# Fourth layer's attention with values standing and turned weights moving, two heads beside each other

## The reference

```python
def odd_mixer(h, w_qkv, q_norm, k_norm, rel_table, w_out):
    q, k, v = jnp.split(h @ w_qkv, 3, axis=-1)
    q = rms_norm_2(split_heads(q, N_HEADS_CHUNK), q_norm)
    k = rms_norm_2(split_heads(k, N_HEADS_CHUNK), k_norm)
    o = chunk_band_attention(q, k, split_heads(v, N_HEADS_CHUNK), rel_table)
    return merge_heads(o) @ w_out

# in chunk_band_attention, for every chunk:
        sc = jnp.einsum('bhqd,bhkd->bhqk', q_c, k_band, preferred_element_type=F32) * scale + bias
        ...
        p = jax.nn.softmax(jnp.where(valid[None, None, None, :], sc, -jnp.inf), axis=-1)
        return jnp.einsum('bhqk,bhkd->bhqd', p.astype(v.dtype), v_band)
```

## Time and profile before

| | us |
|---|---|
| median of 3 runs | 2021.64 |
| lowest, highest | 2015.75, 2021.70 |
| the profiled execution | 2018.59 |
| its span | 2016.8 |
| fourth layer's attention, first scores to the first matmul of the output projection | 620.14 to 646.84 of the span |

### The profile page before, as it was taken

The page is one execution under the profiler, slowest core; times in us unless marked ns, Lnnn a source line. Parts: engine busy times, 40 slices in busy tenths (PEclk is TensorE's granted clock), DMA queues, the critical chain, the costliest instruction groups (busy, mean ns, idle before and its releaser), DMA issues.

```text
span 2016.8 us, 25907 instructions
## 1 busy us (share of the span) xinstructions
PE 1937.1 (96%) x9513; PEld 1597.2 (79%) x9513; DVE 1523.1 (76%) x1723; ACT 1267.1 (63%) x1393; POOL 90.6 (4%) x99
## 2 busy tenths in 40 slices
PE   4999998999999899999999999999999999999997
PEld 3887887888887688888888888888888877778876
DVE  6657765544577789889898888989889884467775
ACT  2544675534455577878777787877778765445553
POOL 0000210000000320000000000000000000100001
PEclk8999998999999999999999999999999999999999
DMA  9774645555552399999999999999999995624400
GB/s 356 238 248 136 211 150 186 178 197 179 170 193 86 130 412 372 379 385 365 386 363 381 374 379 379 362 392 363 381 385 368 379 357 167 209 64 151 169 1 32
DMA packets 186268, 535.12 MB, mean 265 GB/s; under 512 B 12609, under 2 KB 23893, under 8 KB 186198
## 3 DMA queue, kind: packets, MB, share of 16 engines
q1 hardware_dynamic: 179952, 518.95, 70.2%
q10 hardware_dynamic: 4422, 8.92, 1.2%
q0 software_dynamic: 1824, 6.31, 1.2%
HBM read 521.02 MB, written 13.12 MB: 265 GB/s over the span
## 4 chain that ended last, share of the span: by engine, by line
PE 85%; DVE 7%; ACT 4%; DMA 2%; issue 1%; ACTq 0%; DVEq 0%; POOL 0%; SPq 0%
PE bank L456 25%; PE bank L458 24%; PE bank L457 24%; DVE WL L1164 3%; ACT WH L1160 2%; PE bank L654 2%; PE bank L643 1%; DMA ring<-in_od_we_down 1%; PE bank L2706 1%; PE bank L364 1%; DVE P L1148 1%; PE bank L428 1%; PE bank L669 1%; PE bank L667 1%; PE bank L665 1%
## 5 line engine op out<-in xcount | busy, mean ns | idle before, releaser
L1164 DVE TENSOR_TENSOR WL<-ring,WH 128x2048 fp32r<-128x2048 f32 x475 | 1072.0, 2277 | 261.9 <-ACT WH L1160 258.2
L1160 ACT ACTIVATE WH<-ring 128x2048 fp32r<-128x2048 f32 x475 | 901.9, 1912 | 363.8 <-PE bank L458 336.4
L456 PE MATMUL bank<-WH,XTH 128*128 128x512 f32 (+1 forms) x1872 | 740.4, 396 | 16.1 <-DVE XTL L1941 6.5
L458 PE MATMUL bank<-WH,XTL 128*128 128x512 f32 (+1 forms) x1872 | 729.4, 390 | 0.0
L457 PE MATMUL bank<-WL,XTH 128*128 128x512 f32 (+1 forms) x1872 | 729.1, 389 | 0.0
L456 PEld LDWEIGHTS bank<-WH,XTH 128*128 128x128 f32 x1872 | 353.9, 189 | 102.1 <-DVE WL L1164 21.6
L458 PEld LDWEIGHTS bank<-WH,XTL 128*128 128x128 f32 x1872 | 353.7, 189 | 73.9
L457 PEld LDWEIGHTS bank<-WL,XTH 128*128 128x128 f32 x1872 | 354.1, 189 | 68.9 <-issue 0.2
L456 PE MATMUL bank<-WH,HTH 128*128 128x512 f32 (+1 forms) x568 | 219.9, 387 | 1.0 <-DVE WL L1164 0.8
L458 PE MATMUL bank<-WH,HTL 128*128 128x512 f32 (+1 forms) x568 | 217.9, 384 | 0.0
L457 PE MATMUL bank<-WL,HTH 128*128 128x512 f32 (+1 forms) x568 | 217.7, 383 | 0.0
(11 more groups left out here) (442 smaller groups left out, 1371.1 us busy)
## 6 DMA issues: line engine op xcount, KB each, us to landing
ring<-in_od_we_gate SPq DMA_DIRECT2D x112, 1024.0 KB, 7.3
ring<-in_od_we_up SPq DMA_DIRECT2D x112, 1024.0 KB, 8.2
ring<-in_od_we_down SPq DMA_DIRECT2D x112, 1024.0 KB, 8.0
ring<-in_w_in SPq DMA_DIRECT2D x20, 1024.0 KB, 5.7
ring<-in_fox_w_in SPq DMA_DIRECT2D x16, 1024.0 KB, 6.9
ring<-in_nsa_w_in SPq DMA_DIRECT2D x14, 1024.0 KB, 5.1
ring<-in_w_ada SPq DMA_DIRECT2D x12, 1024.0 KB, 10.1
ring<-in_ev_w_in SPq DMA_DIRECT2D x12, 1024.0 KB, 5.2
```

The costliest lines, as they stand in the source:

```text
L456: nc.tensor.matmul(out, x[0], wt[0][:, k, :], start=start, stop=False, skip_group_check=check)
L458: return nc.tensor.matmul(out, x[1], wt[0][:, k, :], start=False, stop=stop, skip_group_check=check)
L1160: nc.scalar.activation(wh, slot_ap(n, nk, width), ACT.Copy).then_inc(hi_made, 1)
L1164: nc.vector.tensor_tensor(wl, slot_ap(n, nk, width), wh.bitcast(F32), ALU.subtract).then_inc(lo_made, 1)
```

## The change

Three things change, all in the fourth layer's attention.

First, the operands of the weighing change places. The values of a head, 128x64, stand as the loaded operand, and its turned weights move: 256 columns for the first 128 keys, 128 for the second. The output is then already turned, with the head's 64 columns on the partitions. The first head of a pair writes partitions 0 to 63 of a bank, the second 64 to 127, so a pair gives one finished slice of 128 rows and 256 tokens of the projection's input. `TO4` goes away: ScalarE copies the slice to XTH (line 817) and VectorE makes XTL (line 841), pair by pair.

Second, the tokens are now on the free axis of the output, so the division can't come after it as one factor per partition. The exponentials are divided before they are turned: VectorE takes the reciprocals of a pair (line 832, signal `inverted`), and GpSimd multiplies the three blocks of each head in place in E (line 824, signal `evened`), two instructions a head. The transposes (line 775) wait for `evened` in place of `exped`.

Third, the lists change. TensorE issues for each p the scores, the transposes of both heads of pair p-1, and then the weighing of pair p-2 (lines 788 and 792). VectorE issues the reciprocals of pair p-1, the maxima of pair p, the copies of pair p-1, and XTL of pair p-3. The output projection is one product over four chunks that waits for the slices.

```diff
+        class TurnedAttention(Attention):
...
+            def turn(self, pe, j):
+
+                pe.wait_ge(evened, j + 1)
+                if j >= 2:
+                    pe.wait_ge(copied, self.u + j - 1)
+                for c in range(3):
+                    last = nc.tensor.transpose(bank[6 + j % 2][:, c * 128:c * 128 + 128],
+                                               self.E[j % 4][:, c * 128:c * 128 + 128], ident[:, :])
+                last.then_inc(turned, 1)
+
+            def weigh_pair(self, pe, p):
+
+                pe.wait_ge(copied, self.u + 2 * p + 2)
+                if p >= 4:
+                    pe.wait_ge(turn_dve, self.bd + p - 3)
+                for kt in range(TT):
+                    for a in range(2):
+                        w_, out = PT[a], bank[p % 4][64 * a:64 * a + 64, :]
+                        if kt == 0:
+                            nc.tensor.matmul(out[:, 0:S], self.units[2 * p + a][2](0),
+                                             w_.rearrange("p (b s) -> p b s", b=3)[:, 0::2, :], start=True, stop=False,
+                                             skip_group_check=True)
+                        else:
+                            nc.tensor.matmul(out[:, 128:S], self.units[2 * p + a][2](1), w_[:, 128:256], start=False,
+                                             stop=True, skip_group_check=True).then_inc(valued, 1)
+
+            def pe(self, pe):
+                N = self.n
+                for p in range(N + 2):
+                    if p < N:
+                        self.scores(pe, p)
+                    if 1 <= p <= N:
+                        for a in range(2):
+                            self.turn(pe, 2 * (p - 1) + a)
+                    if p >= 2:
+                        self.weigh_pair(pe, p - 2)
+
+            def act(self, act):
...
+                    if p >= 3:
+                        act.wait_ge(valued, self.u + 2 * (p - 3) + 2)
+                        nc.scalar.activation(XTH[:, p - 3, :], bank[(p - 3) % 4][:, 0:S], ACT.Copy).then_inc(turn_act, 1)
+
+            def pool(self, pool):
+                for i in range(len(self.units)):
+                    pool.wait_ge(inverted, i // 2 + 1)
+                    for t0, (a, n) in enumerate(((0, 128), (128, 256))):
+                        e = self.E[i % 4][:, a:a + n]
+                        last = nc.gpsimd.tensor_scalar(e, e, rr[:, t0, i % 8:i % 8 + 1], None, ALU.mult)
+                    last.then_inc(evened, 1)
+
+            def dve(self, dve):
+                for p in range(self.n + 3):
+                    if 1 <= p <= self.n:
+                        uu = (2 * p - 2) % 8
+                        dve.wait_ge(exped, self.u + 2 * p)
+                        nc.vector.reciprocal(rr[:, :, uu:uu + 2], rs[:, (p - 1) // 4, :, uu:uu + 2]).then_inc(inverted, 1)
+                    for a in range(2):
+                        if p < self.n:
+                            self.highest(dve, 2 * p + a)
+                    for a in range(2):
+                        if 1 <= p <= self.n:
+                            self.copy(dve, 2 * (p - 1) + a)
+                    if p >= 3:
+                        dve.wait_ge(turn_act, self.ba + p - 2)
+                        nc.vector.scalar_tensor_tensor(out=XTL[:, p - 3, :], in0=bank[(p - 3) % 4][:, 0:S], scalar=1.0,
+                                                       in1=XTH[:, p - 3, :].bitcast(F32), op0=ALU.mult,
+                                                       op1=ALU.subtract).then_inc(turn_dve, 1)
...
-            A4.pe(pe, lambda a: (pe.wait_ge(grouped, A4.g + 1), TO4[0].pe(pe, first=a, end=a + 1)))
-            TO4[0].wait(pe)
-            OUT4[0].pe(pe, last_=False, late=lambda: (A4.wait(pe), TO4[1].pe(pe)))
-            OUT4[1].pe(pe, first=False, operand=TO4[1], closes=True, between=early_tiles(pe, 3, T5))
+            A4.pe(pe)
+            OUT4.pe(pe, operand=A4, closes=True, between=early_tiles(pe, 3, T5))
```

More of the change, by code:

```diff
@@ L750, in bank_of, with __init__, sums, wait_tiles @@
                 return bank[g % 2 * 2 + tt][:, :].rearrange("p (u d) -> p u d", d=self.dv)
+        class TurnedAttention(Attention):
+            def __init__(self, units, bias, bias_ready):
+                self.spare_ready, self.pe_mask = None, None
+                self.units, self.bias, self.bias_ready = units, bias, bias_ready
+                self.E = E + [E_COLS]
+                self.u = base["unit"]
+                self.n = len(units) // 2
+                self.ba, self.bd = base["turn_act"], base["turn_dve"]
+                base["unit"] += len(units)
+                base["turn_act"] += self.n
+                base["turn_dve"] += self.n
+            def sums(self, i, t0):
+                return rs[:, i // 8, t0, i % 8:i % 8 + 1]
+            def turn(self, pe, j):
[32 more added lines that the diff above has]
+                for p in range(self.n + 3):
+                    for i in (2 * p, 2 * p + 1) if p < self.n else ():
+                        act.wait_ge(maxed, self.u + i + 1)
+                        for t0, (a, n) in enumerate(((0, 128), (128, 256))):
+                            e = self.E[i % 4][:, a:a + n]
+                            last = nc.scalar.activation(e, e, ACT.Exp, bias=nmax[:, i % 4, t0:t0 + 1], scale=-1.0,
+                                                        accum_out=self.sums(i, t0))
+                        last.then_inc(exped, 1)
+                    if p >= 3:
[4 more added lines that the diff above has]
+                    pool.wait_ge(inverted, i // 2 + 1)
+                    for t0, (a, n) in enumerate(((0, 128), (128, 256))):
+                        e = self.E[i % 4][:, a:a + n]
+                        last = nc.gpsimd.tensor_scalar(e, e, rr[:, t0, i % 8:i % 8 + 1], None, ALU.mult)
+                    last.then_inc(evened, 1)
+            def dve(self, dve):
+                for p in range(self.n + 3):
+                    if 1 <= p <= self.n:
[13 more added lines that the diff above has]
+                                                       op1=ALU.subtract).then_inc(turn_dve, 1)
+            def wait_tiles(self, eng, n):
+                eng.wait_ge(turn_dve, self.bd + n)
@@ L932, in rel_ready @@
                 dve.wait_ge(rel_set, 4)
-        A4 = Attention([(*head(h), values(2048 + 64 * h, 64)) for h in range(16)], 64, rel_bias,
-                       plain_finish(lambda: A4), bias_ready=rel_ready)
-        TO4, OUT4 = halves_out(c_out3)
+        A4 = TurnedAttention([(*head(h), values(2048 + 64 * h, 64)) for h in range(16)], rel_bias, rel_ready)
+        OUT4 = OutProduct(c_out3, xt, lambda half, tt: bank[4 + 2 * half + tt])
         T5 = Transposes(normed(("od_ffn", 0), X), split=True)
@@ L2131, in _ @@
             dve.wait_ge(r_lo, 1)
[L2132 to L2133 removed]
+            A4.dve(dve)
             nc.vector.memset(stat[:, 60:61], 0.0).then_inc(p_free, 1)
[L2136 to L2140 removed]
+            OUT4.splits(dve)
+            add_to_x(dve, 3, lambda: OUT4.wait(dve), T5, lambda: moe_lo(dve, 0, [0]), lambda: moe_lo(dve, 0, [1]), OUT4.outs)
             dve.wait_ge(iota_set, 2)
```

15 lines of the change are left out of this document (3 added, 12 removed).

## The result

The changed kernel takes 2055.09 us (median of 4 runs, 2052.67 to 2056.47), the kernel before, with one more run beside them, 2018.82 us (4 runs). The ratio is 1.0176, with a 95% interval of 1.0158 to 1.0193. The profiled execution took 2056.47 us, with a mean granted clock of 0.970; before, it was 2018.59 us and 0.986.

The account below looks back on a forecast made before the run. TensorE's own work, 2.90 us a pair, was taken to bound the kernel before. A four-engine chain of 6.16 us a pair gives +24.2 at the full clock, low clock +7.0: +31.2 on 2018.59, or 2050 us; range 2032 to 2060.

Parts of the forecast that it names:

- TensorE's work for a pair: Attention loop: scores 0.86, transposes 0.76 and weighing 0.86 make 2.48 us of TensorE work a pair.
- The ring: Attention loop: closed chain through four engines from one pair's reciprocal to the next, 6.16 us a pair against 2.90.
- GpSimd's price: GpSimd's multiplications in the chain: 0.62 us for 128 columns, 0.94 for 256, 3.08 a pair.
- The quick GpSimd: Rival: GpSimd multiplies at its copy's pace, 2.0 us a pair, kernel 2034 us; chance 0.12.
- The clock: Granted clock falls early in the attention loop: five of eight pairs low, +5.3 us, projection +1.7, together +7.0.
- the sum at the full clock: Whole attention stretch, all eight pairs without low clock: 51.7 us against 26.70, +25.0.
- The projection: Output projection: transposes between chunks go, -0.80 us; its first 3.4 us run at half speed, +1.7.
- Behind the projection: Rest of the program after the output projection: no change in time was put down.
- the main case: Whole kernel: chain with a low clock in part, 2050 us, own range 2045 to 2056; chance 0.52.
- The clock holds: Rival: the same chain in the attention with the clock at 2.4 GHz, kernel 2043 us; chance 0.22.
- Faster: Rival: the chain doesn't bind, TensorE's work sets 2.48 us a pair, -5.6 us, kernel 2013 us; chance 0.04.

Follow-up runs that it names:

- e4: The changed kernel with extra matmuls put into TensorE's holes to hold the granted clock; 2047.76 us, ratio 1.0134 to the kernel before.
- e3: The changed kernel with the weighing of pair p-2 ahead of the transposes of pair p-1 in TensorE's list; 2036.0 us, ratio 1.0070.
- e8: The kernel with shared division, added depth and early projection, plus the first pair divided on VectorE and XTL ahead of the copies; 2017.36 us, ratio 0.9986.
- e10: The kernel of e8 run once more, word for word; 2018.39 us, ratio 0.9989 to the kernel before.

## Why the prediction was right, point by point

**TensorE's work for a pair, 2.48 us: right.** The kernel of the shortened filling goes at 2.47 where nothing holds it up (pair 6: scores at 631.51 us, a weighing at 632.37, transposes at 633.17, the next scores at 633.98). Two small errors cancel in it: the weighing was taken at 0.86 from scores in row halves and is 0.80 at the full clock (also 626.54 to 627.34 in the kernel without division), and the transposes of two heads, taken at 0.76, are 0.81. The matmuls of the two column halves start 6 ns apart (639.516 and 639.522 us in the changed kernel), so they do lie beside each other, as the Trainium skill's page TensorEngine Tiling (Array Packing), Key Properties, says of independent tiles; a drain at the change of mode, which it also names, is too small to be seen in 0.80 us.

**The ring, 6.16 us: right**, 6.02 with the clock held. Term by term: reciprocal 0.17, as taken; signal and reciprocal together 0.26 (649.48 to 649.74) against 0.32; GpSimd 2.98 against 3.08; two copies 0.94 (648.21 to 649.15) against 0.93; XTL 0.33 against 0.35. The other two terms are read at the held clock, in the step of `e4` shown above: the second transposes 0.47 (651.66 to 652.13) against 0.38, and from the weighing to the copy 0.98 against 1.05, by VectorE's row:

```profile
653.11 1.02 DVE L718 COPY scr<-bank 128x384 f32<-128x384 f32 x2 [3.50 <-PE bank L792]
```

The first transposes came 5.49 us after the first scores (620.30 to 625.79), and the prediction's terms give 3.56 + 0.17 + 0.15 + 0.62 + 0.94 + 0.05 = 5.49, to the hundredth by luck. That GpSimd stood last in TensorE's waits would have pointed to GpSimd alone; the thin division and the changed order, which leave everything else as it is, show that the ring was the right unit of the sum, and the added depth agrees.

**GpSimd's price: right, the reason for it weak.** 0.603 and 0.922 us against 0.62 and 0.94 by the slope of two rows. I had taken the row of 2.85 us and not that of 4.07 because of its lighter neighbour. The trace before doesn't bear that out. In the columns of the earlier trace rows, the two at 4.07 us and the two at 2.85 us lie in these stretches:

```profile
238.10:246.24 8.14, 8.14 (x37) 6.75 (x36) 6.42 (x7) 4.99 (x4) 8.13 (x2) 1.00 0.71 200
691.30:696.99 5.69, 5.69 (x27) 4.72 (x26) 4.22 (x10) 3.84 (x2) 5.69 (x2) 1.00 0.54 184
```

VectorE was busy 79% of the first and 74% of the second, and of the two at 2.85 the one that ran half beside a split of 2048 columns took 2.849 us, the other 2.851. Why the other row is slower stays open; that the quick one fitted was in part luck. (The row of 2 columns subtracts a factor per partition and compares; the multiplication of 2 columns took 0.293 in the thin division, so 0.31 was near.) The quick GpSimd, 2034 us, didn't happen. 128 columns more cost 0.32 us, 2.5 ns each. The Trainium skill's GPSIMD Engine Reference, 4.1 Engine selection, has operations with one input near line rate; the trace does not agree here either.

**The clock: the mechanism right, the size too small.** The loss at the low clock, 1.05 us a pair, measured 1.03. But I took five pairs of eight; the granted clock was 0.50 from the first pair's second transposes to 2.7 us into the projection, with one return to 1.00 for 3.4 us at 664. TensorE had been busy 26.8 of the 37.5 us before that return, and 1.08 of 3.30 us within it, before the clock fell again:

```profile
626.50:664.00 37.50, 26.81 (x121) 14.95 (x121) 14.11 (x63) 10.41 (x45) 15.77 (x22) 0.50 0.00 1
```

That makes 58.2 us where 51.7 + 5.3 = 57.0 were predicted. With the holes filled the attention took 52.6 us, 6.8 of them still at 0.50, where a step took 6.95 in place of 6.02. So the low clock cost about 5.6 + 1 = 6.6 us in the attention (an estimate from these), and the sum at the full clock, 51.7, was right. That it "comes back seldom" was said, and then not carried into the count of pairs.

**The projection: +0.3 against +0.9.** The transposes went (-0.80), and the low clock reached only 2.7 us into it.

**Behind the projection: the step that was mis-sized.** I had nothing there; it is 5.9 us. The two rows of the stretch from the router on, at the top, hold the same 6351 matmuls; TensorE is busy 6.6 us longer and stands no longer than before. Slower matmuls mean clock: in that stretch it was at 0.50 for 39 us, against 22 before. The other kernels fit in part: extra low time of 3 to 4 us went with 0.9 to 1.4 us more (without division, the copy first, the added depth, the short filling), 7 us with 2.0, 9 us with 5.0 (`e3`, profiled 5 us above its median), 11 us with 2.6.

How much of this is the chance of one execution can be judged from the kernel of the short filling, which has two profiles. The same code takes 4.0 us longer in the same stretch in the second one, with 35 us at 0.50 against 25:

```profile
664.73:2011.79 1347.06, 1310.71 (x6351) 1076.77 (x6351) 1103.12 (x1124) 934.57 (x916) 61.79 (x57) 0.99 0.81 301
667.57:2018.60 1351.03, 1314.45 (x6351) 1079.09 (x6351) 1103.24 (x1124) 934.35 (x916) 62.44 (x57) 0.99 0.81 300
```

So 5.9 us between two single executions can be chance for the larger part. Against chance alone speak the mean granted clocks of all executions: by these, the four of the changed kernel were at 0.50 for 114 us on average, and 24 of the kernel before for 50. The profiled one had 51 us of it in the attention and the projection; if the others had too, some 13 us (an estimate, give or take 4) are left over for the rest of the program, which at the rates of the two comparisons (5.9 us for 17 us more at 0.50 here, 4.0 for 10 there) is 4 to 5 us. Why a disturbance in the attention should bring more low stretches up to a millisecond later stays open.

Together: 31.5 + 0.3 + 5.9 = 37.7, of the 37.9 us between the two profiled executions; 31.2 was predicted. The sum was 6.5 us short: 1.2 in the attention, 5.9 behind, and -0.6 in the projection. The medians differ by 36.3, so against them it was 5 short: the steps inside the changed stretch came out as worked out, and nothing had been put down for the time behind them. At 2055.1 the kernel lies at the upper edge of the main case's own range, 2045 to 2056.

**The rivals.** "The clock holds" would have been 2043; with TensorE's holes filled the kernel takes 2047.8 us, with 6.8 us at 0.50 still in the attention and low clock behind it. "Faster", 2013 us if the ring didn't bind, was my estimate of the swap's worth, 5.6 us. The runs give 1 to 2.6 us at the medians. From the first scores to the router the kernel of the copy first (without division) has 47.6 us and that of the short filling 47.0 and 48.4, so 3.1, 3.7 and 2.3 below before. What I overlooked is that ScalarE's copy stands in a ring of its own.

## What to carry to other kernels

When a step is put between two others that were one pipeline stage apart, write down the ring through every in-order list that it closes, from one instruction to its own successor, before counting anybody's busy time; its length is the new pace, whatever the engines' shares. If the ring is longer than the busiest engine's work, first move the instruction that closes it, or add a stage: here the same GpSimd work cost 36 us as first ordered, 15 us with the weighing moved, and 6 us with a further step between as well. And once the ring binds, expect holes in TensorE's work to lower its clock, which lengthens the ring again.

## What the runs showed of the hardware

- GpSimd's multiplication by a factor per partition takes 0.293 us for 2 columns, 0.603 for 128 and 0.922 for 256, and these are the same beside a VectorE and a ScalarE that are busy 88% and 75% of the time (the kernel with the added depth). I had allowed for up to a third more.
- ScalarE does such a division of 128 columns in 0.39 us, copying with a scale (the kernel with the division shared):

```profile
640.78 0.39 ACT L833 ACTIVATE P<-P,rr 128x128 f32<-128x128 f32 x1
```

- Profiled executions can be up to 3 us apart before the changed code is reached: the first scores came anywhere from 617.2 to 620.7 us, with a mean granted clock up to there of 0.99 at the early end and 0.97 at the late one. The same kernel profiled twice (`e8`, `e10`) had them at 617.75 and 619.17 us, took 46.98 and 48.40 us from there to the router, and 1347.1 and 1351.0 us behind it. A gain of 3 us must be read from marks inside the stretch, and even there one pause of the clock is worth 1.4 us.
